# Waiting for ScalarE's reads at two places of the retention heads, and moving the wait on the retention gate ahead of the score matmuls

## The reference

```python
h = rmsnorm(x, norm_mix)
rq, rk, rv, rg, aq, ak, av, gate_logits = split(h @ w_in)
q = rotate(rq);  k = rotate(rk) * RET_DK ** -0.5;  v = rv
# both directions of retention together:
out[t] = sum_s gamma(head, direction) ** |t - s| * (q[t] . k[s]) * v[s]
ret_n = out * rsqrt(mean(out * out) + EPS) * ret_norm
branch_a = (silu(rg) * ret_n) @ w_ret_out
# beside it: dilated attention in 3 groups x 8 heads -> branch_b
x = x + (gate_a * branch_a + gate_b * branch_b) @ w_out
x = x + expert_choice_ffn(rmsnorm(x, norm_ffn), ...)   # 16 experts
return rmsnorm(x, norm_final)
```

## Time and profile before

| | |
|---|---|
| runs, median (lowest to highest) | 2621.91 us (2621.75 to 2626.6) |
| the profiled execution: its time, its span | 2621.75 us, 2619.3 us |
| PE busy | 2487.9 us, 95% of the span |
| DVE, ACT, POOL busy | 1596.8, 1375.3, 386.7 us |
| DMA, mean | 210 GB/s |
| mean granted TensorE clock | 0.98 |

### The profile page before, as it was taken

One profiled execution on the slowest core, in us unless ns is written; L12 is line 12 of the kernel. 1 busy time (PEld: TensorE's weight loads), 2 busy tenths in 40 slices (PEclk: granted clock), 3 DMA queues, 4 the chain that ended last, 5 costly groups with the idle time before them and its releaser, 6 DMA issues.

```text
span 2619.3 us, 39067 instructions
## 1 busy us (share of the span) xinstructions
PE 2487.9 (95%) x13778; PEld 2148.7 (82%) x13778; DVE 1596.8 (61%) x1885; ACT 1375.3 (53%) x1512; POOL 386.7 (15%) x313
## 2 busy tenths in 40 slices
PE   7999999999979999999999399999999999999994
PEld 6998989788869998897788388888888888888883
DVE  3444444432334444444323588888888888888884
ACT  3434343432234343435332277777777777777774
POOL 2313122110113131221101200000000000000000
PEclk9999999999989999999999699999999999999997
DMA  4212121123232121211233699999999999999994
GB/s 165 88 37 86 48 88 49 57 81 144 97 131 80 57 88 48 88 48 58 81 117 114 237 376 384 385 386 382 389 385 391 384 377 393 380 381 394 385 373 172
DMA packets 129981, 550.22 MB, mean 210 GB/s; under 512 B 9088, under 2 KB 9216, under 8 KB 119664
## 3 DMA queue, kind: packets, MB, share of 16 engines
q1 hardware_dynamic: 122592, 522.81, 52.4%
q0 software_dynamic: 7312, 26.39, 3.4%
HBM read 528.20 MB, written 20.97 MB: 210 GB/s over the span
## 4 chain that ended last, share of the span: by engine, by line
PE 91%; DVE 3%; issue 2%; ACT 2%; DMA 1%; POOL 0%; SPq 0%; DVEq 0%; ACTq 0%; POOLq 0%
PE bank L946 40%; PE bank L705 30%; PE bank L721 10%; PE bank L736 4%; PE bank L820 2%; PE bank L975 2%; PE bank L757 1%; PE bank L788 1%; PE bank L768 1%; PE bank L809 1%; PE bank L910 1%; PE bank L793 1%; DVE w_lo L1402 1%; DMA w_raw<-in_w_b 0%; DVE y_tile L1849 0%
## 5 line engine op out<-in xcount | busy, mean ns | idle before, releaser
L1771 DVE TENSOR_TENSOR m_lo<-m_raw,m_hi 128x2048 fp32r<-128x2048 f32 x381 | 869.9, 2291 | 123.5 <-ACT m_hi L1307 121.6
L1307 ACT ACTIVATE m_hi<-m_raw 128x2048 fp32r<-128x2048 f32 x384 | 737.4, 1921 | 266.3 <-PE bank L946 266.3
L705 PE MATMUL bank<-w_hi,h_hi 128*128 128x256 f32 (+1 forms) x1536 | 490.3, 319 | 3.5 <-DVE h_lo L1578 1.8
L705 PE MATMUL bank<-w_hi,h_lo 128*128 128x256 f32 (+1 forms) x1536 | 475.1, 309 | 0.0
L705 PE MATMUL bank<-w_lo,h_hi 128*128 128x256 f32 (+1 forms) x1536 | 474.7, 309 | 0.0
L946 PE MATMUL bank<-m_hi,xs_hi 128*128 128x512 f32 x1040 | 324.1, 393 | 1.4 <-DVE xs_lo L1793 1.4
L946 PE MATMUL bank<-m_lo,xs_hi 128*128 128x512 f32 x1040 | 321.1, 390 | 0.0
L946 PE MATMUL bank<-m_hi,xs_lo 128*128 128x512 f32 x1040 | 321.1, 390 | 0.0
L705 PEld LDWEIGHTS bank<-w_hi,h_hi 128*128 128x128 f32 x1536 | 291.5, 190 | 32.1 <-issue 28.3
L705 PEld LDWEIGHTS bank<-w_lo,h_hi 128*128 128x128 f32 x1536 | 292.0, 190 | 0.0
L705 PEld LDWEIGHTS bank<-w_hi,h_lo 128*128 128x128 f32 x1536 | 291.5, 190 | 0.0
(11 more groups left out here) (188 smaller groups left out, 3466.0 us busy)
## 6 DMA issues: line engine op xcount, KB each, us to landing
m_raw<-in_w_exp_gate SPq DMA_DIRECT2D x128, 1024.0 KB, 7.9
m_raw<-in_w_exp_up SPq DMA_DIRECT2D x128, 1024.0 KB, 6.5
m_raw<-in_w_exp_down SPq DMA_DIRECT2D x128, 1024.0 KB, 7.4
w_raw<-in_w_b SPq DMA_DIRECT2D x24, 1536.0 KB, 6.4
w_raw<-in_w_a SPq DMA_DIRECT2D x24, 1024.0 KB, 4.8
w_raw<-in_w_c SPq DMA_DIRECT2D x24, 1024.0 KB, 4.8
w_raw<-in_w_d SPq DMA_DIRECT2D x8, 1024.0 KB, 4.9
xt<-in_x SPq DMA_DIRECT2D x8, 512.0 KB, 5.7
```

The lines of the kernel that those rows point to most:

```text
L705: last = pe.matmul(ps_proj[:, proj.slot, 0:cols], a[:, c, tokens], v[:, c, :], start=c == n == 0, stop=c == chunks - 1 and n == 2)
L1307: act.activation(m_hi[slot.slot][:, :, :], m_raw[raw.slot][:, :, :], ACT.Copy)\
L1771: dve.tensor_tensor(m_lo[slot.slot][:, :, :], m_raw[raw.slot][:, :, :], m_hi[slot.slot][:, :, :].bitcast(F32), ALU.subtract)\
```

## The change

Three waits of TensorE change. No instruction that computes or moves data is added or taken away, and the other engines' programs are the same.

- At D0 TensorE waits for every transpose so far, also for the latest, R(None,0).
- At K0 it waits for every transpose so far, where it let the latest three be unread.
- The wait on `s_swish`, the Silu over the gate, stands at K0 in place of O0.

```diff
@@ step D of attention_step
                     if r == 0:
 
-                        all_read(pe, s_tr_free, tr, but=1)
+                        all_read(pe, s_tr_free, tr)
                     all_read(pe, s_sc_free, sc)
@@ step K of retention_step
                     if j == 0:
 
-                        all_read(pe, s_tr_free, tr, but=3)
+                        all_read(pe, s_tr_free, tr)
+                        pe.wait_ge(s_swish, ret.n(1))
                     pe.wait_ge(s_sc_free[sc.slot], START + sc.lap)
@@ step O of retention_step
                     if i == 0:
                         all_read(pe, s_sc_free, sc)
-                        pe.wait_ge(s_swish, ret.n(1))
                     pe.wait_ge(s_out_free[outs.slot], START + outs.lap)
```

## The result

The changed kernel takes 2658.77 us at the median of its four runs (2658.12 to 2659.88), and 1.0144 times the kernel before, with a 95% interval of 1.0130 to 1.0157. In all 23 executions of the changed kernel are on record with this result, from 2657.76 to 2664.98 us. One execution of the kernel before, of 6276.16 us, lies far outside; it is left out of the ratio but still counted in the recorded median of 2624.26 us (2621.91 without it; later rounds have 2622.8 and 2624.23). Of 2624.26 us the ratio makes 37.8 us more (34.1 to 41.2). Forecast were 30.85 us, so the direction and the place were right and the size was a fifth too low.

The account below looks back on a forecast made before the run. TensorE was taken as the bound, busy 434.77 of 436.00 us in the first batch's heads and attention. Terms 18.9 + 5.6 + 1.1 + 5.25 = 30.85 us on 2621.75 gave 2652.6 us, range 2644 to 2660.

Parts of the forecast that it names:

- TensorE as the bound, with nothing to win back in the loops: First batch's heads and attention: TensorE busy 434.77 of 436.00 us, so holds in the loops lengthen the kernel fully.
- K0 in the loops: Six K0 places, each held for ScalarE's R(0,1) copy plus hand-over: 6 x 3.15 = 18.9 us (17.4 to 20.4).
- D0, 5.6 us: Eight D0 places, each waiting for ScalarE's copy of R(None,0): 8 x 0.70 = 5.6 us (4.0 to 6.8).
- The fourth head, 1.1 us: K0 twice held some 1.5 us by the Silu, partly taken up at O0: 0.55 each, 1.1 us (0 to 3.0).
- The Silu's wait taken from O0: At O0, removing the wait gives back 0, since O0 never waited for the Silu.
- The clock: Behind the six loop holds, three dips to 1.2 GHz: 3 x 1.75 = 5.25 us, between none and six (10.5).
- The rival without dips: At the loop holds the clock stays at full rate; only the holds cost, 25.6 us: 2647.4 us; chance 0.12.
- a wait taken up later: Holds come off later waits behind each batch's heads: 2624 us; chance 0.03 together with no effect.
- a faster kernel: At O0 and O2 TensorE stops waiting because a later K0 suits VectorE better: 2618 us; chance 0.01.
- no effect: At K0 and D0 ScalarE had read the transposes anyway: 2621.9 us; chance 0.03 together with taken up later.
- The clock low for long: Behind each of the six loop holds, half of 10 us lost, 30 us on top of 25.6: 2677 us; chance 0.03.
- The third rival: Behind each batch's heads, ten later waits (11.6 us) take up the holds: 2624 us; chance 0.03 together with no effect.

Follow-up runs that it names:

- the filled kernel: Changed kernel plus throwaway matmuls on TensorE ahead of K0's waits (12; 6 in the fourth head): ratio 1.0100 to the kernel before, 26.2 us more.
- a fourth execution: The changed kernel run a fourth time with no further edit: ratio 1.0128 to the kernel before, profiled execution 2659.35 us.

## What the prediction had right, and the step that failed

- **TensorE as the bound, with nothing to win back in the loops:** right. The holds of 26.6 us are in the time at full length (26.2, between 22.3 and 30.4, by the filled kernel). The loads and the other engines moved along.
- **K0 in the loops, 18.9 us:** right, at 6 x 3.25 = 19.5. ScalarE's copy for R(0,1) releases it, the Silu ends just ahead. The hand-over was 0.33 us and not 0.2, still inside the bounds. That the price is ScalarE's order was shown from both sides: with the copy moved ahead it is gone, with the Silu longer by 1.38 us the hold is longer by 1.38.
- **D0, 5.6 us:** right, 8 x 0.73 = 5.8, and 6.8 (4.5 to 9.2) when measured alone.
- **The fourth head, 1.1 us:** right in mechanism: K0 held 1.59, O0's wait gone, part of it given back; 1.3 us for both. The wait at O2 grew by 0.19 us, where the prediction had it smaller.
- **The Silu's wait taken from O0:** right in that it gives nothing back; but two projections lie between K0 and O0, where the working says three.
- **The clock, "I expect three such dips of the six places: 3 x 1.75 = 5.25 us":** this is the step that failed, a term that was mis-sized. It counted dips behind the six holds and put the clock of the rest of the kernel at no change. For the profiled execution the count and the price were about right: three dips, 4.4 us of time. One execution in two of the trace's pair of waits is a thin ground for it, though, and three was partly luck: a fourth execution had four places and five dips' worth, and other kernels with holds of 2.6 to 3.0 us lost the clock at five or six of six places, some for twice as long. That a single hold can cost two dips lay outside the bound of "none and six (10.5)". Over the runs the clock costs 12.6 us between the changed and the filled kernel (the intervals of the two ratios leave some 7 to 18). Of the 12.4 us between their traces, 4.6 lie with the holds and 7.8 elsewhere: at the start, which can be chance, and in the stages behind the heads, where the first batch's routing lost one more dip in all four profiled executions. Forecast and result differ by 37.8 - 30.85 = 7 us, and this term by 12.6 - 5.25 = 7.4.
- **The rival without dips** (2647.4) fell for the changed kernel, whose traces have three or four holds with a dip; it is what the filled kernel shows, 2648.66 us at its median. The Trainium skill's advice against idle gaps between bursts of matmuls (TensorE: Matmul & The Clock Gate, "Why this matters for your kernels") was weighed as speaking for that rival. The gaps of 3.0 and 3.1 us agree with it, with the clock lost at six and at three or four of six places. The gaps of 2.6 us don't: they are shorter than what it warns of and lost the clock at five of six, and here the measurement decides.
- **The rivals of a wait taken up later, of a faster kernel and of no effect** fell: only the fourth head's wait at O0 was of the kind that stays, as the working said. The clock low for long fell too; no hold was followed by more than twice the time of a short dip. The third rival counts ten waits and 11.6 us behind each batch's heads; the list has ten rows, but one of them stands for three waits, and its totals add up to 12.0 us. Half of 25.6 is 12.8 us and not 12.6. Neither changes what the rival says.

What stays open is where the longer executions lose their clock, behind the holds or elsewhere, and why the changed kernel loses it behind the unchanged waits of the first batch's routing.

## What to carry to other kernels

Before a wait is made stricter, find the youngest operation that it now asks for and read what stands ahead of that in its engine's queue: the wait costs the distance to that queue's end of it, whatever the data need. Reordering the releasing engine by one step, into time in which it idles anyway, can take the whole price away. On an engine at its limit, expect that a hold as long as those here (2.6 us and more) also costs clock, and don't take the clock in the rest of the kernel as fixed: here the clock made the change half as dear again as the holds (12.6 us beside 26.2), and in the one pair of traces that splits it, about two thirds of that lay away from them.

## What the runs showed of the hardware

- TensorE loses its clock behind single waits of 2.6 to 3.1 us in the middle of an otherwise full stretch: at 5 of 6 places (2.6 us), 6 of 6 (3.0), 3 or 4 of 6 (3.1) and 6 of 6 (4.5), mostly for 1.7 to 1.8 us of full speed missing, 1.4 to 1.6 us of time in the changed kernel's trace, and sometimes for twice that. Eight waits of 0.7 us and two of 1.5 us did nothing to it.
- The same pair of waits of 1.90 and 0.92 us lost the clock in one batch of two in the kernel before and in the filled kernel, in both batches in all four executions of the changed kernel, and in neither in the kernel with the longer Silu; a loss is 1.6 us.
- Throwaway matmuls of 2.92 us during a 3.25 us hold kept it at 2.4 GHz at all six places, and the kernel was 12.6 us faster than with idle holds, of which 4.6 of 12.4 us lie at the holds in the traces.
- The restart of a held TensorE takes 0.20 us (D0) and 0.33 us (K0) from the end of ScalarE's row to the weight load.
- A Silu over 128x1024 cut into 16 calls of 64 columns takes 2.44 us in place of 1.06, some 0.09 us for each further call.
